# A hybrid decoder step on one core: the projection phase of the RWKV-7 layer goes over three token groups

## What is computed

```
h_prev = concatenate([prev, h[:, :-1]]);  xx = h_prev - h
xs = h + xx * mu            # six mixes: r, k, v, w (decay), a (rate), g (gate)
r, k, v = xs[0] @ Wr, xs[1] @ Wk, xs[2] @ Wv          # each 1024 x 1024
w_log = -softplus(-(w0 + tanh(xw @ w1) @ w2)) - 0.5   # w1: 1024 x 64, w2: 64 x 1024
decay = exp(-exp(w_log))
a = sigmoid(a0 + (xa @ a1) @ a2)                      # a1: 1024 x 64
g = sigmoid(xg @ g1) @ g2                             # g1: 1024 x 160
```

## Time and profile before

| | us |
|---|---|
| median of 3 runs | 4023.01 |
| profiled execution, its own time | 4022.81 |
| its span | 4021.0 |
| TensorE busy | 3431.7 (85%) |
| VectorE busy | 1906.7 (47%) |
| GpSimd busy | 1565.9 (39%) |
| ScalarE busy | 1345.6 (33%) |
| mean granted clock of TensorE | 0.911 |

### The profile page before, as it was taken

The page is one execution under the profiler, slowest core; times in us unless marked ns, Lnnn a source line. Parts: engine busy times, 40 slices in busy tenths (PEclk is TensorE's granted clock), DMA queues, the critical chain, the costliest instruction groups (busy, mean ns, idle before and its releaser), DMA issues. The chain is left out here.

```text
span 4021.0 us, 78382 instructions
## 1 busy us (share of the span) xinstructions
PE 3431.7 (85%) x34057; PEld 3122.6 (78%) x34057; DVE 1906.7 (47%) x2166; ACT 1345.6 (33%) x2067; POOL 1565.9 (39%) x648
## 2 busy tenths in 40 slices
PE   5999695898988268999999999866886889999896
PEld 2899444888888268999999999844555889999896
DVE  3222705455542559337254443089843953512622
ACT  1111122343332124333333343344554433333332
POOL 0111000000000044665656666465402556556563
PEclk8999957899999589999999999978897999999998
DMA  5222024343332163444445466567845344444442
GB/s 193 84 84 79 17 106 145 104 133 120 120 118 77 60 199 102 132 141 139 138 127 150 141 192 184 167 205 252 312 147 163 110 121 137 122 144 141 124 140 69
DMA packets 710476, 546.84 MB, mean 136 GB/s; under 512 B 34762, under 2 KB 667490, under 8 KB 709884
## 3 DMA queue, kind: packets, MB, share of 16 engines
q1 hardware_dynamic: 664182, 473.18, 38.3%
q10 hardware_dynamic: 45606, 67.55, 4.8%
q0 software_dynamic: 352, 1.18, 0.1%
HBM read 471.55 MB, written 70.29 MB: 135 GB/s over the span
## 5 line engine op out<-in xcount | busy, mean ns | idle before, releaser
L1630 POOL TENSOR_TENSOR dense_w_lo<-dense_w_raw,dense_w_hi 128x1024 fp32r<-128x1024 f32 x504 | 1273.5, 2533 | 972.8 <-ACT dense_w_hi L1701 970.6
L1686 PE MATMUL acc<-dense_x_hi,dense_w_hi 128*128 128x344 f32 x2496 | 813.7, 330 | 85.9 <-DVE dense_x_lo L1791 41.6
L1687 PE MATMUL acc<-dense_x_lo,dense_w_hi 128*128 128x344 f32 x2496 | 803.0, 326 | 0.0
L1701 ACT ACTIVATE dense_w_hi<-dense_w_raw 128x1024 fp32r<-128x1024 f32 x504 | 531.2, 1056 | 627.0 <-PE acc L1691 533.8
L1686 PEld LDWEIGHTS acc<-dense_x_hi,dense_w_hi 128*128 128x128 f32 x2496 | 482.9, 193 | 98.2 <-issue 79.6
L1687 PEld LDWEIGHTS acc<-dense_x_lo,dense_w_hi 128*128 128x128 f32 x2496 | 483.0, 193 | 2.5 <-issue 0.9
L1686 PE MATMUL acc<-dense_hid_hi,dense_w_hi 128*128 128x344 f32 x1536 | 483.3, 319 | 0.5 <-DVE dense_hid_lo L1811 0.5
L1687 PE MATMUL acc<-dense_hid_lo,dense_w_hi 128*128 128x344 f32 x1536 | 483.4, 319 | 0.0
L1691 PE MATMUL acc<-dense_x_hi,dense_w_lo 128*128 128x344 f32 x2496 | 448.7, 322 | 1.7 <-POOL dense_w_lo L1630 1.7
L1691 PEld LDWEIGHTS acc<-dense_x_hi,dense_w_lo 128*128 128x128 f32 x2496 | 408.9, 190 | 2.6 <-POOL dense_w_lo L1630 2.6
L750 POOL TENSOR_TENSOR x0T<-nT,levels 128x512 f32<-128x512 f32 x16 | 29.7, 1855 | 748.2 <-DVE bR L1249 748.2
(11 more groups left out here) (385 smaller groups left out, 5922.5 us busy)
## 6 DMA issues: line engine op xcount, KB each, us to landing
dense_w_raw<-in_ffn_w SPq DMA_DIRECT2D x384, 512.0 KB, 4.1
ada_quarter<-in_ada_w SPq DMA_DIRECT2D x40, 1024.0 KB, 10.6
att_k_page<-in_cache_k SPq DMA_DIRECT2D x64, 512.0 KB, 4.2
att_v_page<-in_cache_v SPq DMA_DIRECT2D x64, 512.0 KB, 5.5
scratch_mix<-proj_stage ACTq DMA_DIRECT2D x48, 516.0 KB, 2.7
scratch_mix<-dense_stage ACTq DMA_DIRECT2D x72, 172.0 KB, 2.1
w_raw<-in_a_w_rkv SPq DMA_DIRECT2D x24, 512.0 KB, 4.1
dense_w_raw<-in_a_w_o SPq DMA_DIRECT2D x24, 512.0 KB, 4.4
```

Of the source, the lines that this page charges most:

```text
L1630: nc.gpsimd.tensor_tensor(wlo[:, i % NW], raw[:, i % NRAW], whi[:, i % NW].bitcast(F32), ALU.subtract).then_inc(S("lo"), 1)
L1686: T_.matmul(out, whi[:, s % NW, k, :], a, start=j.first and k == 0, stop=False)
L1687: T_.matmul(out, whi[:, s % NW, k, :], b, start=False, stop=False)
L1701: A(whi[:, i % NW], raw[:, i % NRAW], ACT.Copy).then_inc(S("hi"), 1)
```

## The change

`project_phase` is rewritten; the two-slab ring and its helpers go away, and the input phase no longer makes `xx`. `h` gets a zero column in front, so that a group's difference is one subtraction of shifted views, and it is made per group in the projection phase.

- The outer loop is over the three token groups. Within a group the uses come in the order r, w, k, a, g (with its tail t), then the second stage for this group, then v. So every weight slab is loaded and split three times, 84 instead of 28.
- Three mix buffers of 8 x 344 columns (NX = 3). A use waits for the matmuls of the use three before it. All mixes but the very first are made as eight mix operations and then one high and one low operation over 2752 columns.
- Weights: four raw buffers (NRAW), three of high and low parts (NW). For a slab TensorE waits for the high part only, does 16 high matmuls, then waits for the low part and does 8 low ones. ScalarE makes the high part of slab s+2 before it takes slab s.
- Six PSUM banks are used one by one (NB = 6), each by one output of 128 x 344.
- The rate's w1 slab is loaded twice, side by side to 128 columns, so that its result also lies in partitions 64 to 127. Decay's and rate's second-stage weights share one tensor of 128 partitions, decay in the first 64, rate in the last 64; per `mo` there is a decay and a rate product, in two banks, and then the gate's two. The scaling of the decay moves from VectorE to GpSimd.
- Four output slots of 2 x 344 columns; two outputs go out in one store.
- TensorE's loops are written out; before, the middle slabs were in hardware loops.

```diff
-            nc.vector.tensor_tensor(xx[:, :, 1:SEQ], h[:, :, 0:SEQ - 1], h[:, :, 1:SEQ], ALU.subtract)
...
+        NRAW, NW, NB, NX, NOUT = 4, 3, 6, 3, 4
+        ORDER = "rwkagv"
+        WIDTH = {"r": P, "k": P, "v": P, "w": 64, "a": P, "g": P, "t": 32}
...
+        for g in range(NG):
+            for i, kind in enumerate(ORDER):
+                use = len(ORDER) * g + i
+                if kind in "rkv":
+                    for mo in range(KC):
+                        un = unit() if mo % 2 == 0 else un
+                        add(kind, g, mo, use, 1, un)
+                elif kind == "g":
+                    add("g", g, 0, use, 1, -1)
+                    add("t", g, 0, use, 1, -1)
+                    for mo in range(KC):
+                        add("wa", g, mo, -1, 2, unit())
+                        ug = unit() if mo % 2 == 0 else ug
+                        add("gg", g, mo, -1, 1, ug)
+                else:
+                    add(kind, g, 0, use, 1, -1)
...
         @block.sync
+            for s in range(NS_):
+                need(sp, "lo", s - NRAW + 1)
+                for cols, src in weights(slabs[s]):
+                    nc.sync.dma_start(raw[:, s % NRAW, :, cols], src).then_inc(S(f"w_in{s % NRAW}"), 16)
...
         @block.gpsimd
+            for i, j in enumerate(jobs):
+                if j.slab >= 0:
+                    s, w = j.slab, WIDTH[j.kind]
+                    need(pool, "hi", s + 1)
+                    if s >= NW:
+                        need(pool, "mm", mms[slab_job[s - NW]])
+                    nc.gpsimd.tensor_tensor(wlo[:, s % NW, :, 0:w], raw[:, s % NRAW, :, 0:w],
+                                            whi[:, s % NW, :, 0:w].bitcast(F32), ALU.subtract).then_inc(S("lo"), 1)
+                if j.kind == "wa":
+                    need(pool, "taken", taken[j.accs[0]])
+                    lw = stage[:, j.unit % NOUT, 0, :]
+                    nc.gpsimd.tensor_scalar(lw, lw, DECAY_SCALE, None, ALU.mult).then_inc(S("decay"), 1)
...
         @block.tensor
+            for i, j in enumerate(jobs):
+                for a in j.accs:
+                    if a >= NB:
+                        need(pe, "taken", taken[a - NB])
+                if j.slab >= 0:
+                    s, w, x = j.slab, WIDTH[j.kind], j.use % NX
+                    out = bank(j.accs[0])[0:w, :]
+                    need(pe, "hi", s + 1)
+                    if use_start[j.use] == s and j.use > 0:
+                        need(pe, "x_mix", KC + j.use)
+                    for k in range(KC):
+                        if s == 0:
+                            need(pe, "x_mix", k + 1)
+                        T_.matmul(out, whi[:, s % NW, k, 0:w], xh[:, x, k, :], start=k == 0, stop=False)
+                        T_.matmul(out, whi[:, s % NW, k, 0:w], xl[:, x, k, :], start=False, stop=False)
+                    need(pe, "lo", s + 1)
+                    for k in range(KC):
+                        last = T_.matmul(out, wlo[:, s % NW, k, 0:w], xh[:, x, k, :], start=False, stop=k == KC - 1)
+                elif j.kind == "wa":
+                    cols = slice(j.mo * P, j.mo * P + P)
+                    T_.matmul(bank(j.accs[0]), w2wa[0:64, cols], lwa[0:64, :], start=True, stop=True)
+                    last = T_.matmul(bank(j.accs[1]), w2wa[64:P, cols], lwa[64:P, :], start=True, stop=True)
+                else:
+                    T_.matmul(bank(j.accs[0]), w2g[:, cols], lg[:], start=True, stop=False)
+                    last = T_.matmul(bank(j.accs[0]), w2t[:, cols], lt[:], start=False, stop=True)
...
         @block.vector
+                last = V.tensor_tensor(xx[:, :, 0:n], h1[:, :, c0:c0 + n], h, ALU.subtract)
...
+                    for k in range(KC):
+                        last = V.scalar_tensor_tensor(tmp[:, k, :], xx[:, k, :], m.vec(V_MU + MIX[kind], k),
+                                                      h1[:, k, 1 + c0:1 + c0 + G], ALU.mult, ALU.add)
...
+                        if use >= NX:
+                            need(dve, "mm", mms[slab_job[use_end[use - NX]]])
+                        V.tensor_copy(xh[:, x], tmp[:]).then_inc(S("x_hi"), 1)
+                        need(dve, "x_hi", KC + use)
+                        V.tensor_tensor(xl[:, x], tmp[:], xh[:, x].bitcast(F32), ALU.subtract).then_inc(S("x_mix"), 1)
...
         @block.scalar
+            high(0)
+            high(1)
+            for i, j in enumerate(jobs):
+                if 0 <= j.slab < NS_ - 2:
+                    high(j.slab + 2)
+                need(act, "mm", mms[i])
...
+                if j.kind == "wa":
+                    for q in range(2):
+                        A(stage[:, slot, q, :], bank(j.accs[q]), ACT.Sigmoid, bias=m.vec(V_W0 + q, j.mo)).then_inc(S("taken"), 1)
+                    need(act, "decay", wa_nth[i] + 1)
```

More of the change, by code:

```diff
@@ new lines, in project_phase @@
+        slabs = [j for j in jobs if j.slab >= 0]
+        NS_ = len(slabs)
+        use_end = {j.use: j.slab for j in slabs}
+        use_start = {}
+        for j in slabs:
+            use_start.setdefault(j.use, j.slab)
+        taken = {}
+        for j in jobs:
+            for a in j.accs:
+                taken[a] = len(taken) + 1
+        mms = {}
+        for i, j in enumerate(jobs):
+            mms[i] = i + 1
+        s2_first = {g: [i for i, j in enumerate(jobs) if j.kind == "wa" and j.g == g][0] for g in range(NG)}
@@ new lines, in project_phase, with bank, weights @@
+        s2_last = {g: [i for i, j in enumerate(jobs) if j.kind == "gg" and j.g == g][-1] for g in range(NG)}
+        slab_job = {j.slab: i for i, j in enumerate(jobs) if j.slab >= 0}
+        wa_nth = {i: n for n, i in enumerate(i for i, j in enumerate(jobs) if j.kind == "wa")}
+        lora_in = {(j.kind, j.g): taken[j.accs[0]] for j in jobs if j.kind in ("a", "t")}
+        def bank(a):
+            return m.acc[a % NB // 3][:, a % NB % 3, 0:G]
+        def weights(j):
+            if j.kind in "rkv":
+                return [(slice(0, P), slab_of(io["a_w_rkv"][0, MIX[j.kind]], j.mo))]
+            if j.kind == "a":
+                return [(slice(q, q + 64), slab_of(io["a_a1"][0], 0, 64)) for q in (0, 64)]
+            w = WIDTH[j.kind]
+            return [(slice(0, w), slab_of(io["a_w1" if j.kind == "w" else "a_g1"][0], 1 if j.kind == "t" else 0, w))]
@@ L460, in _, with landed @@
+        def landed(s):
+            return sum(16 * len(weights(slabs[i])) for i in range(s % NRAW, s + 1, NRAW))
         @block.sync
         def _(sp):
-            for j in range(3):
-                w = io["a_w_rkv"][0, j]
-                for q in range(2):
-                    ring_load(m, sp, slab_of(w, q), s0 + j * KC + q, q, first=(j == 0 and s0 == 0))
-                with sp.Fori(1, KC // 2) as i:
-                    for q in range(2):
-                        ring_load(m, sp, slab_at(w, i * 2 + q), i * 2 + (s0 + j * KC + q), q)
@@ L491, in _ @@
         @block.tensor
         def _(pe):
-            for j in range(3):
-                for q in range(2):
-                    ring_mul(m, pe, s0 + j * KC + q, q, xh, xl, first=(j == 0 and s0 == 0),
-                             ready=(mix_l, KC * j) if q == 0 else None)
-                with pe.Fori(1, KC // 2 - 1) as i:
-                    for q in range(2):
-                        ring_mul(m, pe, i * 2 + (s0 + j * KC + q), q, xh, xl)
-                for q in range(2):
-                    ring_mul(m, pe, s0 + j * KC + KC - 2 + q, q, xh, xl, free=x_free if q else None)
@@ L502, in _ @@
[L502 to L521 removed]
+            T_ = nc.tensor
@@ L594, in _, with high @@
-            for p in range(2):
-                act.wait_ge(out_done[p], 16 * 12)
-                act.wait_ge(out2[p], 16 * 12)
-        m.slabs = sL + NL
+            A = nc.scalar.activation
+            def high(s):
+                w = WIDTH[slabs[s].kind]
+                act.wait_ge(S(f"w_in{s % NRAW}"), landed(s))
+                if s >= NW:
+                    need(act, "mm", mms[slab_job[s - NW]])
+                A(whi[:, s % NW, :, 0:w], raw[:, s % NRAW, :, 0:w], ACT.Copy).then_inc(S("hi"), 1)
@@ L600, in scan_phase @@
+            for i in range(NOUT):
+                act.wait_ge(S(f"out{i}"), 16 * len(range(i, state["unit"], NOUT)))
 def scan_phase(m):
```

297 lines of the change are left out of this document (106 added, 191 removed).

## The result

The changed kernel takes 3905.07 us in the median of 4 runs (3897.22 to 3917.18), the kernel before 4023.37 beside it: a ratio of 0.9698, 95% interval 0.9678 to 0.9718. Run twice more it gave 3911.64 and 3906.33 us (0.9703 [0.9683, 0.9723] and 0.9709 [0.9688, 0.9729]). The gain is 118 us where 84 were forecast.

A forecast was written before the change was run, and what follows sets the result against it. The projection phase was held bound by TensorE's waits for mixed tokens and a low-clock second stage. Terms 86.8 + 27.5 + 313.7 + 11.5 + 84 + 6 + 4.3 = 533.8 against 617.3 saved 83.5: 3939 us, range 3906 to 3978.

The forecast's parts named there:

- the second stages: Decay, rate and gate products after each group's first-stage uses: 28 us a group, 84 in all, clock falling after 11.6 us.
- the stalls of the first group: TensorE waiting for the mixes of k (6.5 us) and g (5) in the first token group: 11.5 us, between 0 and 30.
- the rest of the kernel: Everything after the projection phase was to stay unchanged; a move above 5 us would make the sum wrong.
- v's first low parts: v's first weight subtraction, queued on GpSimd behind the last decay: 2 us a group, 6 in all (0 to 12).
- Start and end: Projection phase starts at 86.8 us, 3.2 earlier; at its end 4.3 us to the next phase instead of 5.2.
- First slab: Slab 1 takes 27.5 us from phase start: first mix, three weight subtractions delaying VectorE by 7.2, and low-clock matmuls.
- Slab pitch and weight stream: First stage after slab 1: 83 slabs at 3.78 us, 313.7 in all, with the three-fold weight loading and splitting hidden.
- Rivals C and D: C: VectorE and GpSimd become the bound, 3963 us, chance 0.13; D: three-fold weight stream sets the pitch, 4083, chance 0.03.
- the chain of ScalarE: Second stage: sigmoids, copy, issues and decay wait, 3.1 us a chunk, 25 a group at 2.4 GHz, setting the pace.
- Rival A: Second stage stays at 2.4 GHz, decays hardly wait: 60 us instead of 84, stalls 5; kernel 3909 us, chance 0.14.

The follow-up runs named there:

- the mixed version of the old kernel: Kernel before, with its 24 second-stage units alternating decay, rate, gate per output chunk instead of eight of each in a row: 3976.71 us, ratio 0.9872.
- the last version: Changed kernel with low parts of v's first two slabs before the decays, and ScalarE storing rate and decay after the gate's copy: 3890.33 us, ratio 0.9639.

## Why the prediction was wrong

The forecast was 3939 us, the range 3906 to 3978, the time 3905: the sign was right, the size was 34 us short. Three steps failed: the second stages were put at 84 us and took 63.1 (a fall of the clock that didn't come, and a wait for the decay priced too high), the stalls of the first group at 11.5 and took 0.5, and the rest of the kernel was held unchanged and got some 13 us shorter. A fourth, v's first low parts, took 20.4 for 6 and hid 14 us of this: that the phase as a whole is only 22 us off is in part luck. By its steps:

*Start and end*: right (86.1 for 86.8; last slab 503.7 to the next phase 511.6, 4.1 after its 3.8 us, for 4.3).

*First slab*: the mechanism was right, the size 4 too large. VectorE's timeline:

```profile
86.11 3.02 DVE L517 TENSOR_TENSOR proj_xx<-h 128x2752 f32<-128x2752 f32 x1 [6.12 <-PEq L92]
...
90.59 0.57 DVE L527 SCALAR_TENSOR_TENSOR proj_mix<-proj_xx,vecs,h 128x344 f32<-128x344 f32 x1
91.19 0.34 DVE L532 CAST proj_x_hi<-proj_mix 128x344 fp32r<-128x344 f32 x1
91.57 0.52 DVE L534 TENSOR_TENSOR proj_x_lo<-proj_mix,proj_x_hi 128x344 fp32r<-128x344 f32 x1
92.00 0.57 DVE L527 SCALAR_TENSOR_TENSOR proj_mix<-proj_xx,vecs,h 128x344 f32<-128x344 f32 x1
92.61 2.38 DVE L532 CAST proj_x_hi<-proj_mix 128x344 fp32r<-128x344 f32 x1
```

A chunk is 1.41 us (90.59 to 92.00), not 1.54, and each of the three weight subtractions adds 2.0, not 2.4: each holds one operation of VectorE, as 0.34 becomes 2.38 when GpSimd starts at 92.39. That makes the mix 2 us shorter. The last 2 us are those that I had added for a slab 1 at the low clock: slab 1 takes 3.78.

*Slab pitch and weight stream*: right. 3.78 in every steady slab, the weights' split hidden at three times the amount (GpSimd 50.48 of 72.40 us). Rivals C and D are excluded.

*First-group stalls*: mis-sized, 11.5 for 0.5. VectorE and GpSimd then:

```profile
106.72 3.99 DVE L527 SCALAR_TENSOR_TENSOR proj_mix<-proj_xx,vecs,h 128x344 f32<-128x344 f32 x8
110.75 1.59 DVE L541 CAST proj_x_hi<-proj_mix 128x2752 fp32r<-128x2752 f32 x1
112.38 5.11 DVE L543 TENSOR_TENSOR proj_x_lo<-proj_mix,proj_x_hi 128x2752 fp32r<-128x2752 f32 x1
117.53 12.45 DVE L527 SCALAR_TENSOR_TENSOR proj_mix<-proj_xx,vecs,h 128x344 f32<-128x344 f32 x8
```
```profile
111.29 3.32 POOL L465 TENSOR_TENSOR proj_w_lo<-proj_w_raw,proj_w_hi 128x1024 fp32r<-128x1024 f32 x1 [9.21 <-ACT proj_w_hi L554]
```

I gave VectorE 1.38 us per slab from the end of slab 0 on. But it ends r's mix at 106.7, before slab 1, and GpSimd, which has made three low parts ahead, is idle for 9.21 us until 111.29: w's mix ran almost unhindered and was ready at 117.5, where 8.7 us at 1.38 a slab would have ended near 130. After that a mix takes 18.1, 19.3 and 19.2 us (ready at 135.6, 155.0 and 174.1), where the forecast's share makes 8.7 / 1.38 x 3.78 = 23.8. So VectorE gets about 1.74 us a slab beside GpSimd and not 1.38; why isn't shown, but it isn't the third buffer of split weights, without which nothing changed. k was ready 4 us before TensorE wanted it, g 0.3 after.

*Second stage*: the largest error, 84 for 63.1. At 2.4 GHz the forecast had 25 us a group, so 9 of the 20.9 us are the clock and 12 the chain of ScalarE. The clock I let fall after 11.6 us because it had fallen there before. What I took for a property of long second-stage work was one of its order, as the mixed version of the old kernel shows. Rival A had the outcome (60 us), at a chance of 0.14, but its argument, more rows of the array at work per us, is only half borne out: a chunk in turn uses 72 rows on average in the mixed version and keeps 1.00, the old decay and rate products used 64, but the old gate pairs used 80 and, coming after the fall, stayed at 0.50 for 69.3 us. Per chunk TensorE needs 2.33 us, as worked out (2.4), the pair side by side. ScalarE's chain was worked out as 3.1 a chunk and was to set the pace; the stages took 2.85, 2.67 and 2.36, the last being TensorE's own. The wait of each decay for VectorE, which I averaged at 0.8, comes only where a long operation of VectorE meets one (in the first stage the decays take 1.27 us in the median): the first decay of the first stage takes 3.69 us, beside a VectorE subtraction of 3.02; in the third stage VectorE is idle. The Trainium skill, "SBUF — State Buffer", section "Who interferes with whom", has a VectorE instruction with two inputs in SBUF contend with a GpSimd instruction that reads SBUF. The subtraction and the scaling are such a pair, and the 3.69 us against 1.07 for a decay beside an idle VectorE agree.

```profile
183.24 3.02 DVE L517 TENSOR_TENSOR proj_xx<-h 128x2752 f32<-128x2752 f32 x1
...
183.51 3.69 POOL L470 TENSOR_SCALAR proj_stage<-proj_stage 128x344 f32<-128x344 f32 x1 [8.78 <-ACT proj_stage L580]
```

*v's first low part*: right in mechanism, 6 for 20.4. I let TensorE run two chunks ahead of ScalarE and priced only a weight subtraction; it was the last decay itself that came 4 us after v's first matmul, and TensorE's idle time then cost a low clock besides (0.50 for 3.4 us, and 6.8 and 3.4 in the other groups). The experiment with the low parts ahead of the decays shows it; that the last decay came so late was in part the 1.67 us for the output slot, which I had put at nothing.

*"Everything after the phase unchanged"*: wrong by some 13 us in the medians, by 20 in the profiled run. The phase itself would have given 3939 - 22 = 3917, inside the range; the rest carried the time out of it, to 3905. Its cause stays open.

## What to carry to other kernels

When a stretch runs at the low clock, look at the order of the array heights in it before its length: interleaving products of few rows with full ones cost nothing and gave 49 us of the phase here, though a clock that is high by it can still fall after waits, as in one stage of the last version. Count an engine's free time for a new dependency from when it ends its last work, buffers filled ahead included, and in a queue shared by two consumers put first the one that the busiest engine will want first. Double the buffer that a slow producer refills; the next one after that is worth little (91 us, then 11).

## What the hardware showed unexpectedly

A run of 48 products of 64 rows, and then alternating pairs of 128 and 32 rows, are granted 0.50 from 504.6 to the end of the stage, 107.5 us; the same products with the heights in turn are granted 1.00 for 69 us. Which of the two old stretches would fall by itself wasn't tried. A short stand-still of TensorE (4.6 us from 207.6) is followed by 3.4 us at 0.50, so a wait costs more than itself: with one mix buffer 74 us of added idle time made 103. Identical code of 790 us scatters from 776 to 797 us between programs, and 8 us between repeats of one.
